# RWKV chunks as two interleaved streams with ScalarE taking the copies, and one block for constants, loads and turning at the front

## The reference, cut to what matters

```python
def _rwkv7_scan(r, w, k, v, kk, a, S0):
    def step(S, inp):
        rt, wt, kt, vt, kkt, at = inp
        sa = jnp.einsum('bhvk,bhk->bhv', S, -kkt)
        S = S * wt[:, :, None, :] + sa[..., None] * (kkt * at)[:, :, None, :] + vt[..., None] * kt[:, :, None, :]
        return S, jnp.einsum('bhvk,bhk->bhv', S, rt)
```

## Time and profile before

| | |
|---|---|
| time, median of 3 runs (lowest to highest) | 5399.87 us (5395.56 to 5401.0) |
| profiled execution: its time, its span | 5405.28 us, 5403.6 us |
| busy over the span: TensorE, VectorE, ScalarE | 4808.1, 2903.1, 1537.5 us |
| granted TensorE clock, mean of the span | 0.927 |
| front, to the start of the first norm | 0 to 38.3 us |
| first norm with 8 modulation units | 38.3 to 83.3 us |
| RWKV chunks, 8 rounds | 786.5 to 1127.6 us |

### The profile page before, as it was taken

One profiled execution on the slowest core, in us unless ns is written; L12 is line 12 of the kernel. 1 busy time (PEld: TensorE's weight loads), 2 busy tenths in 40 slices (PEclk: granted clock), 3 DMA queues, 4 the chain that ended last, 5 costly groups with the idle time before them and its releaser, 6 DMA issues. The chain is left out here.

```text
span 5403.6 us, 59892 instructions
## 1 busy us (share of the span) xinstructions
PE 4808.1 (89%) x23383; PEld 3888.6 (72%) x23383; DVE 2903.1 (54%) x4345; ACT 1537.5 (28%) x2935; POOL 1338.4 (25%) x571
## 2 busy tenths in 40 slices
PE   6996647659999999999999797779999999999998
PEld 4665326647788887788888664657788887788886
DVE  1043454442588874266666103932877973466665
ACT  1010200001255565222222101411265563222222
POOL 0000000000244444444444000000433444444442
PEclk9996757879999999999999896889999999999999
DMA  4231100003355677555553214023465586455552
GB/s 143 78 102 59 42 16 1 1 33 93 95 163 166 181 217 204 182 191 193 189 197 138 94 47 134 7 87 95 128 177 169 163 240 204 166 197 189 192 191 92
DMA packets 531707, 709.98 MB, mean 131 GB/s; under 512 B 47625, under 2 KB 415874, under 8 KB 510434
## 3 DMA queue, kind: packets, MB, share of 16 engines
q1 hardware_dynamic: 526004, 689.08, 40.1%
q0 software_dynamic: 4608, 16.78, 0.9%
q10 hardware_dynamic: 814, 0.29, 0.0%
HBM read 552.62 MB, written 149.21 MB: 130 GB/s over the span
## 5 line engine op out<-in xcount | busy, mean ns | idle before, releaser
L2182 PE MATMUL ps<-h_parts,u_parts 128*128 128x512 f32 x6144 | 1431.7, 393 | 24.1 <-PEq L1681 13.3
L2433 PE MATMUL ps<-w_parts,v_parts 128*128 128x512 f32 x6144 | 1398.4, 390 | 14.7 <-DVE w_parts L2418 14.7
L2433 PEld LDWEIGHTS ps<-w_parts,v_parts 128*128 128x128 f32 x6144 | 1157.2, 188 | 255.9 <-POOL v_parts L2404 15.5
L2182 PEld LDWEIGHTS ps<-h_parts,u_parts 128*128 128x128 f32 x6144 | 1151.9, 189 | 261.8 <-POOL u_parts L1659 13.8
L1659 POOL TENSOR_TENSOR u_parts<-u_turned,u_parts 128x1024 fp32r<-128x1024 f32 x256 | 663.6, 2593 | 2211.1 <-ACT u_parts L1654 2210.9
L2418 DVE TENSOR_TENSOR w_parts<-w_rows,w_parts 128x512 fp32r<-128x512 f32 x256 | 625.3, 2443 | 481.9 <-ACT w_parts L2397 481.9
L197 PE MATMUL ps<-h,arena 128*128 128x264 f32 (+2 forms) x2176 | 485.9, 387 | 80.8 <-DMA arena<-in_even_w_out_dram 33.4
L2404 POOL TENSOR_TENSOR v_parts<-u_rows,v_parts 128x1024 fp32r<-128x1024 f32 x172 | 413.0, 2402 | 539.9 <-ACT v_parts L2395 539.9
L197 PEld LDWEIGHTS ps<-h,arena 128*128 128x128 f32 (+1 forms) x2176 | 411.3, 189 | 155.9 <-DMA arena<-in_even_w_out_dram 33.8
L1960 DVE TENSOR_TENSOR onehots<-iota,choice 128x1024 f32<-128x1024 f32 x256 | 381.3, 1529 | 193.8 <-PE ps L2214 193.4
L1646 DVE STREAM_TRANSPOSE u_turned<-u_rows 128x1024 f32<-128x1024 f32 x256 | 317.2, 1239 | 237.2 <-POOL u_parts L1659 215.8
(11 more groups left out here) (489 smaller groups left out, 4325.2 us busy)
## 6 DMA issues: line engine op xcount, KB each, us to landing
u_rows<-in_peer_u_dram SPq DMA_DIRECT2D x1024, 128.0 KB
u_rows<-in_peer_v_dram SPq DMA_DIRECT2D x86, 1024.0 KB, 4.9
hidden_tiles<-hidden SPq DMA_DIRECT2D x256, 256.0 KB
gate_matrices<-h SPq DMA_DIRECT2D x64, 1024.0 KB, 7.4
gates<-gate_matrices SPq DMA_DIRECT2D x32, 2048.0 KB, 7.9
u_turned<-hidden_tiles SPq DMA_DIRECT2D x256, 256.0 KB, 3.4
v_rows<-in_peer_v_dram SPq DMA_DIRECT2D x42, 1024.0 KB, 4.8
arena<-in_ada_w_dram SPq DMA_DIRECT2D x40, 1024.0 KB, 5.3
```

Source lines behind the costliest of these rows:

```text
L2182: ins = mm(ps[:, n % 2, :], q.uTs[:, n % 3, wp, k, :], q.hs[:, xp, k, :], start=k == 0 and (wp, xp) == (0, 0), stop=k == DT - 1 and wp == 1)
L2433: ins = nc.tensor.matmul(ps[:, o, :], q.vs[:, n % 3, vp, o * P:(o + 1) * P], q.ws[:, n % 3, wp], start=n == 0 and (vp, wp) == (0, 0), stop ...
```

## The change

**Chunks.** One block holds all eight rounds. Heads are split in two streams, `x` = 0 and 1, each of two heads (one 128-partition tile), each with four banks of its own and its own three semaphores (`chain_pe`, `chain_dve`, `chain_act`). A round of a stream has 16 steps. The lists of each engine are written by `alternate`: one step of stream 0, then one step of stream 1 that is 8 steps (`CHAIN_LAG`) behind. Every bank is 256 columns wide in use where it was 512, so there are twice as many VectorE or ScalarE operations of half the width. ScalarE takes the plain copies (`tok`, `X2`, `X4`, `M8`, `LV`, `M2` of the joins, `GU`, `y`, `Bm`), VectorE the masks and the sums, and the copies `M2`, `M4` and `X2` of the joins. VectorE waits for its own earlier results only where it reads them.

**Front.** `constants` is gone; its work and that of the load block move into the block of `tiles_stage` through `begin`. SyncE issues x first, then the conditioning rows, then four modulation loads (`FRONT_MODS`); the other four are issued by SyncE in the block of `mix_norm`. TensorE turns x as soon as x and `ident` are there, and the rows last, waiting for them there. VectorE drains all of x's banks, ScalarE both of the rows'. `rows` is set to zero first, and ScalarE's loads and the conditioning rows wait for that.

```diff
-    for quad in range(8):
-        with nc.Block() as block:            # each round: step_pe / step_dve, all four heads at once
...
+CHAIN_PE, CHAIN_DVE, CHAIN_ACT = 22, 16, 10
+CHAIN_LAG = 8
...
+    def products(pe, x):
+        mm, b = nc.tensor.matmul, 4 * x
...
+            def both(bank, lhs, rhs):
+                for i in range(2):
+                    ins = mm(ps[:, b + bank, i * P:(i + 1) * P], lhs[:, i, :], rhs[:, i, :], start=True, stop=True)
+                ins.then_inc(made.sem, 1)
...
+            if quad:
+                act_of(0)
+            for j, src in enumerate((e.kt, e.ke, e.be, xb[:, 8:12, :])):
+                ins = nc.tensor.transpose(ps[:, b + 3, j * P:(j + 1) * P], src[:, tile, t], s.ident[:])
+            ins.then_inc(made.sem, 1)
+            yield                                             # step 1
+            if quad:
+                dve_of(0)
+            inner(0, e.kt, e.bh)
+            inner(P, e.bh, e.kt).then_inc(made.sem, 1)
+            yield                                             # step 2
+            dve_of(2)
+            both(2, w.X, w.M)
+            act_of(1)
+            both(3, w.M, w.X)
+            yield                                             # step 3
+            dve_of(3)
+            inner(0, e.bh, xb)
+            inner(P, e.kh, e.kt).then_inc(made.sem, 1)
+            yield                                             # step 4
+            dve_of(4)
+            act_of(2)
+            both(2, w.X2, w.M2)
+            both(3, w.M2, w.X2)
+            yield                                             # step 5
+            dve_of(5)
+            inner(0, e.kh, xb).then_inc(made.sem, 1)
+            yield                                             # step 6
+            act_of(3)
+            both(3, w.M2, w.R)
+            dve_of(6)
+            both(2, w.X4, w.M4)
+            yield                                             # step 7
+            dve_of(8)
+            both(0, w.M4, w.R2)
+            yield                                             # step 8
+            act_of(4)
+            dve_of(9)
+            both(1, w.M8, w.R)
...
+            yield                                             # step 9
+            dve_of(10)
+            turned(3)
+            both(0, w.O1, w.R2)
+            yield                                             # step 10
+            act_of(6)
+            dve_of(11)
+            both(1, w.M2, w.X2)
+            yield                                             # step 11
...
+    def sums(dve, x):
...
+            pe_of(2)
+            done(masked(w.M, 0, 0))
+            done(masked(w.X, P, 3))
+            masked(w.O1, 0, 1)
+            masked(w.O2, 0, 2)
+            own(2)
+            done(v.tensor_tensor(w.R, w.X, s.ident[:].unsqueeze(1).to_broadcast([P, 2, P]), ALU.add))
+            yield
+            pe_of(3)
+            done(v.tensor_copy(w.M2, w.bank(2)))
+            yield
...
+            pe_of(15)
+            done(v.tensor_copy(w.X2, w.bank(0)))
+            yield                                             # step 10
...
+    def copies(act, x):
...
+            pe_of(1)
+            done(a.copy(w.tok, ps[:, b + 3, :].rearrange("p (j c) -> p j c", j=4)))
...
+            pe_of(20)
+            done(a.copy(w.GU, w.bank(1)))
...
+    def alternate(stream, engine):
+        first, second = stream(engine, 0), stream(engine, 1)
+        for step in range(8 * 16 + CHAIN_LAG):
+            next(first, None)
+            if step >= CHAIN_LAG:
+                next(second, None)
...
+FRONT_MODS = 4
...
+    def load_x(sp):
+        for dst, src in first:
+            sp.dma_start(dst, src).then_inc(s.x_loaded.sem, 16)
+        sp.wait_ge(s.consts.sem, s.consts.at(1))
+        for dst, src in early:
+            sp.dma_start(dst, src).then_inc(s.loaded.sem, 16)
+        for i in range(FRONT_MODS):
+            mods.load(sp, i)
+
+    def load_rest(act):
+        act.wait_ge(s.consts.sem, s.consts.at(1))
...
+    def x_there(pe):
+        pe.wait_ge(s.consts.sem, s.consts.at(3))
+        pe.wait_ge(s.x_loaded.sem, s.x_loaded.at(16 * len(first)))
...
+        @block.sync                                           # in mix_norm
+        def _(sp):
+            for i in range(FRONT_MODS, mods.count if mods else 0):
+                mods.load(sp, i)
```

More of the change, by code:

```diff
@@ L113, in give, with tiles_stage @@
             self.arena.give(self.places.pop(i)[1])
[L121 removed]
+def tiles_stage(s, groups, banks=1, blocks=(), kt=DT, ahead=None, begin=None):
     nc = s.nc
@@ L332, in load_rows @@
               (s.m_s[:], io["state_mlstm_m"].rearrange("o b h -> h (o b)"))]
[L333 to L355, removed]
+    begin = State()
+    def dve_first(dve):
+        nc.vector.memset(rows[:], 0.0).then_inc(s.consts.sem, 1)
+        nc.vector.memset(s.ones[:], 1.0)
+        nc.vector.memset(s.ones512[:], 1.0).then_inc(s.consts.sem, 1)
@@ new lines, in load_x @@
+    def load_x(sp):
[8 more added lines that the diff above has]
+        act.wait_ge(s.consts.sem, s.consts.at(1))
+        with nc.allow_non_contiguous_dma("two small states of a few values each"):
+            for dst, src in loads:
+                act.dma_start(dst, src).then_inc(s.loaded.sem, 16)
@@ L361, in load_rows, with rows_turned, fill_there @@
                                                   ps[:, 0:DT * B].rearrange("p (k b) -> p k b", k=DT))))
-    tiles_stage(s, groups)
+    def rows_turned(g, n):
+        b, fill, engine, drain = transposes(
+            s, [(rows[:, 4 * g + i, :], i * P) for i in range(n)], "act",
+            lambda eng, ps: copy(eng, nc, s.cols[:, 4 * g:4 * g + n, :], ps[:, 0:n * P].rearrange("p (a b) -> p a b", a=n)))
+        def fill_there(ps, w):
+            nc.tensor.wait_ge(s.loaded.sem, s.loaded.at(16 * (len(early) + len(loads))))
+            return fill(ps, w)
+        return (b, fill_there, engine, drain)
+    groups += [rows_turned(1, ROW_TILES - 4), rows_turned(0, 4)]
+    tiles_stage(s, groups, begin=begin)
+    s.consts.close(3)
+    s.x_loaded.close(16 * len(first))
+    s.loaded.close(16 * (len(early) + len(loads)))
 def col(s, name, i=0, n=1):
@@ new lines, in alternate, with _ @@
+    def alternate(stream, engine):
[4 more added lines that the diff above has]
+                next(second, None)
+        assert next(first, 0) == 0 and next(second, 0) == 0
+    with nc.Block() as block:
+        @block.tensor
+        def _(pe):
+            alternate(products, pe)
+        @block.vector
+        def _(dve):
+            alternate(sums, dve)
+        @block.scalar
+        def _(act):
+            alternate(copies, act)
```

378 lines of the change are left out of this document (194 added, 184 removed).

## The result

The changed kernel takes 5269.74 us (median of 4 runs, 5266.05 to 5273.29) against 5400.43 of the kernel before (4 runs, 5395.56 to 5402.56): ratio 0.9759, 95% interval 0.9742 to 0.9776. The forecast was 5269.

A forecast was written before the change was run, and what follows sets the result against it. Waits in a strict relay between engines, not an engine itself, bound both stages. Profiled 5405.3 us minus 110 (chunks) and 21 (front) gave 5274; the median stood 5.4 lower, so 5269, range 5240 to 5325.

The forecast's parts named there:

- The two savings: Whole kernel: chunks go from 341.1 to 231 us, saving 110; the front ends at 17 instead of 38.3, saving 21.
- The lone start: Chunks: stream A alone for its first eight steps, 8.1 us at full clock, plus 4 for half clock.
- the joint rounds: Chunks: 15 half rounds of 13.35 us with both streams, 200.3, plus 5 until TensorE's clock is lifted.
- the lone end: Chunks: stream B alone for its last eight steps, 12.1 us at full clock, plus 2.
- The order of a half round: Chunks: TensorE start times, stream A at steps 2 to 9, B at 10 to 16 and 1; A10 at 13.2 us.
- So a round is 26.7 us, of which TensorE issues 21.2: Chunks: two half rounds, 13.2 and 13.5 us, laid out in program order; products alone take 21.2.
- the other waits are 0.1 to 0.4 us: Chunks, half round: TensorE's waits apart from the one long wait, at B11 behind VectorE's masks and R.
- the terms +4 and +5: Chunks' start: 4 us for the lone stretch at half clock, 5 more until TensorE's clock is lifted.
- The rival of the swinging clock: Chunks: TensorE at half clock for part of 15 half rounds; 5328 us for half, 5299 for a quarter; chance 0.16.
- Half clock and the gaps stay: Chunks: TensorE never lifted, waits of 2.7 us per half round stay; stage 388 us, whole 5426; slower, chance 0.04.
- the change doesn't do it: Chunks at half clock without gaps, 347 us, and a front saving only 6: whole 5400; no change, chance 0.02.
- the TensorE-bound rival: Chunks: TensorE never waits, half rounds of 10.6 us; whole 5218; chance 0.06 for under 5240.

The follow-up runs named there:

- VectorE alone: Changed kernel with VectorE also making ScalarE's copies, two streams, lag 8 and one block kept: 5275.97 us, ratio 0.9777.
- the three profiles with an earlier rise: Profiles of the changed kernel with VectorE making all copies (5275.97 us), masks one step later (5260.31), eight front loads (5271.09); first eight steps 12.0 to 12.2 us.

## Why the prediction came out right, and which term was wrong

- **The two savings.** The chunks: 227.8 us measured, 231 predicted. The front: 20.2 of 21, 17 (10 to 24) when tried alone. The sum had 131 us, the profiles show 132.0, after a loss of 1.5 behind the chunks that the sum didn't have. These three errors (a saving forecast 3.3 too small, 0.8 and 1.5 too large) partly cancel. That the forecast was met within 1 us is luck: the four runs of the kernel alone spread over 7 us.

- **The terms of the stage.** The lone start was 14.2 us (8.1 + 4 predicted), the joint rounds 200.7 (200.3 + 5), the lone end 12.9 (12.1 + 2). So the 227.8 against 231 hide an error of 2 in one direction and of 6 in the other.

- **The order of a half round.** The starts on TensorE, from A2:

| | B10 | A3 | B11 | A4 | B12 | A6 | B14 | A10 |
|---|---|---|---|---|---|---|---|---|
| predicted | 0.5 | 1.7 | 3.3 | 3.8 | 4.6 | 6.6 | 7.5 | 13.2 |
| measured | 0.64 | 1.57 | 2.96 | 3.60 | 4.25 | 6.40 | 6.98 | 12.96 |

The other half took 26.58 - 12.96 = 13.6 (13.5 predicted), the round 26.58 (26.7).

- **The step that was mis-sized: "So a round is 26.7 us, of which TensorE issues 21.2".** The ledger filled the other 5.5 us with waits. In the half shown above its own starts give 0.55 at A3, 0.7 at B11, 0.3 at B12, 0.6 at B14 and 0.3 at B16, so that "the other waits are 0.1 to 0.4 us" doesn't fit them either. The starts of the weight loads in the round 861.42 to 888.00 have 2.4 us of waits: five gaps between products of one kind, 0.31 to 0.50 each and 2.1 in all, and 0.3 beyond the usual gap at three changes of kind. The step had no term for the changes themselves: TensorE goes from products that use the whole array to those that use a part of it, from these back, or from one kind of part to another, 19 times in a round at lag 8, by the order of its list. At 0.19 each this is 3.6 us. TensorE's own 21.2 was somewhat too large as well: it has 2.2 for the twelve outputs of 64 partitions, which took 1.75 at lag 8 and 1.55 at lag 0, so that 20.8 and 20.6 are left. The sums of the three terms, each from its own rows:

| | products | changes | waits | sum | measured |
|---|---|---|---|---|---|
| lag 8 | 20.8 | 19: 3.6 | 2.4 | 26.8 | 26.58 |
| lag 1 | 20.8 | 14: 2.7 | 1.5 | 25.0 | 25.16 |
| lag 0 | 20.6 | 9: 1.7 | 2.5 | 24.8 | 24.77 |

The waits of lag 1 and lag 0 are counted in the same way. At lag 8 and lag 0 they are nearly the same, so what lies between the two rounds (1.8 us) is, within the error of the sums, the ten changes (1.9). The sums close within some 0.2 us, which is about one change. The forecast had the waits 3 us too long and the changes at nothing, and the two errors cancelled: that the round came out at 26.7 is luck. VectorE's masks were costed too dear as well: 0.33 to 0.36 us apart (1.42 for four) instead of 0.39, and A3 waited 0.3 instead of 0.5.

- **ScalarE and VectorE not the bound.** Right, 58.0 and 117.7 us busy (55 to 65 and "about 125" foreseen); and by more than the text said, since VectorE alone loses 0.85 us a round. ScalarE's 128-wide copy, set at 0.29, is 0.27 (266 ns in the mean of 16).

- **The clock.** Right that it stays at 1.00 once the streams run together. The start cost 6.2 us (5.0 alone and 1.2 in the first joint half, against the run with TensorE warm; about 3 by the three profiles with an earlier rise) where the terms +4 and +5 stood for 9. That the clock rises when there are no gaps, which the prediction read from the earlier trace rows, isn't what those rows show: TensorE was busy 1.83 of 2 us at 0.50 and 0.43 of 2 us at 1.00. The run with TensorE warm shows that unused products ahead of the stage give 1.00 from its first step; what else lifts it was not tried. The rival of the swinging clock was false, and no run with two interleaved streams showed it. It is true for the same work without the interleaving. "Half clock and the gaps stay" and "the change doesn't do it" were false; the TensorE-bound rival (5218) wasn't reached by any kernel, since it knew nothing of the changes of kind: with nine of them in a round, its half round of 10.6 would be 11.5, without any wait.

- **The front.** x was there at 10.3 us (9 to 10), the block ended at 18 (17), no unit waited for its weights. That SyncE's issues would set the block's end with eight loads in it is shown (6.2 us later). What it costs in the whole is not: 1.4 us, within the measurement. The start of SyncE's last four loads in the norm's block costs nothing that the windows show (45.0 us before and after).

## What to carry over

Where a stage is a relay between engines, put a second, independent chain into its gaps before moving copies to an idle engine: here the interleaving was worth all of the stage's gain and the idle engine's part some 6 us of it. Once TensorE is the one that never waits, count in its list how often full-array and part-array products alternate, and choose the offset between the chains that keeps like ones together; half a round, the offset with the shorter waits behind the masks, was the worse one here. Test an offset by its constant: lag 0, 1, 8 and 128 gave 5240, 5242, 5270 and 5403 us (ratios 0.9702, 0.9716, 0.9759 and 1.0012).

## What was not expected of the hardware

- Each change between a full-array product and one of 64 rows, or of 64 output columns, holds TensorE's issue for 0.19 us at full clock, without a record of its own; it looks like an idle gap of 0.17 to 0.20 us with "issue" behind it, or like nothing.
- The same relay of two-product steps ran at a mean clock of 0.78 when its gaps were left open, and 40 us of it at 0.50; with the gaps filled it had 1.00 as long as both streams ran.
- A gain or a loss in one stage reached the end only in part: the norm 6.2 us later gave 1.4 us (eight loads in front), and 0.6 us of the chunks' gain was lost in the next stage, which TensorE began at half clock. Behind it the distance between the profiles before and after moved up and down by some 2 us. This was seen in single profiles and not followed further.
